# Branch projections of a hybrid encoder layer: another order of weight sums and gate loads, and a sum moved to VectorE

## The reference

```python
y_a = o_a @ w_proj_a[l]      # o_a, o_b: 512 x 1024;  w_proj_a, w_proj_b: 1024 x 2048
y_b = o_b @ w_proj_b[l]
merged = jax.nn.sigmoid(gate_a) * y_a + jax.nn.sigmoid(gate_b) * y_b
x = x + merged @ w_out[l]
```

## Time and profile before

| | us |
|---|---|
| median of 3 runs | 2690.0 |
| the runs | 2689.77 to 2694.65 |
| span of the profiled execution, first to last instruction | 2690.4 |
| TensorE busy in it | 2647.6 (98%) |
| VectorE, ScalarE, GpSimd busy in it | 1820.0, 1374.9, 540.6 |

### The profile page before, as it was taken

How to read it: one execution, slowest core, us unless ns; L and a number is a source line. 1 busy time by engine, 2 the same in 40 slices (tenths; PEclk the granted TensorE clock), 3 DMA queues, 4 the chain that set the end, 5 groups by cost and what they waited for, 6 DMA issues and landing times.

```text
span 2690.4 us, 33239 instructions
## 1 busy us (share of the span) xinstructions
PE 2647.6 (98%) x12726; PEld 2195.0 (82%) x12726; DVE 1820.0 (68%) x2116; ACT 1374.9 (51%) x1692; POOL 540.6 (20%) x390
## 2 busy tenths in 40 slices
PE   8999999999999989999999999999999999999998
PEld 7888888888888778778887888888888888888887
DVE  5865555777666768788458555666655568778787
ACT  6544444645546654545455444444444445544446
POOL 7121112000023222211241122111112212121311
PEclk9999999999999999999999999999999999999999
DMA  8887887532232299875358888787787888798975
GB/s 275 213 196 198 193 184 176 149 89 80 82 92 73 83 256 242 212 200 137 98 157 219 175 170 173 173 198 170 170 179 167 177 213 194 196 208 237 187 213 133
DMA packets 323681, 466.79 MB, mean 174 GB/s; under 512 B 30840, under 2 KB 139728, under 8 KB 320976
## 3 DMA queue, kind: packets, MB, share of 16 engines
q0 software_dynamic: 88672, 170.94, 36.9%
q1 hardware_dynamic: 231936, 288.33, 33.7%
q10 hardware_dynamic: 2928, 5.56, 0.6%
HBM read 430.43 MB, written 34.34 MB: 173 GB/s over the span
## 4 chain that ended last, share of the span: by engine, by line
PE 69%; DVE 4%; DMA 4%; issue 4%; ACT 1%; POOL 1%; DVEq 0%; ACTq 0%; POOLq 0%
PE psum L1186 12%; PE psum L1188 12%; PE psum L1187 12%; PE psum L1607 9%; PE psum L1608 9%; PE psum L1609 9%; DMA f_raw<-in_w_down 1%; PE psum L1369 1%; PE psum L1860 1%; PE psum L1567 1%; PE psum L1568 1%; PE psum L1569 1%; DMA m_tot<-in_w_proj_a 1%; DVE f_lo L3331 1%; DMA out_last<-in_w_out 0%
## 5 line engine op out<-in xcount | busy, mean ns | idle before, releaser
L3552 DVE TENSOR_TENSOR f_lo<-f_raw,f_hi 128x1024 fp32r<-128x1024 f32 x458 | 558.9, 1223 | 398.6 <-ACT f_hi L2572 397.5
L2572 ACT ACTIVATE f_hi<-f_raw 128x1024 fp32r<-128x1024 f32 x460 | 486.6, 1060 | 620.8 <-PE psum L1609 309.8
L1140 POOL DMA_DIRECT2D f_raw<-in_w_up x132 | 158.9, 1204 | 662.3 <-DVE f_lo L3552 619.7
L2893 DVE TENSOR_TENSOR fr_lo<-fr_raw,fr_hi 128x1024 fp32r<-128x1024 f32 x140 | 171.2, 1224 | 158.1 <-ACT fr_hi L2024 157.9
L2024 ACT ACTIVATE fr_hi<-fr_raw 128x1024 fp32r<-128x1024 f32 x140 | 148.4, 1061 | 197.9 <-PE psum L1321 99.7
L1059 POOL TENSOR_TENSOR w_lo<-w_raw,w_hi 128x1024 fp32r<-128x1024 f32 x55 | 136.8, 2502 | 534.6 <-ACT w_hi L1950 526.3
L1186 PE MATMUL psum<-op_hi,w_lo 128*128 128x512 f32 x576 | 233.5, 405 | 0.0
L1188 PE MATMUL psum<-op_hi,w_hi 128*128 128x512 f32 x576 | 224.9, 391 | 0.0
L1187 PE MATMUL psum<-op_lo,w_hi 128*128 128x512 f32 x576 | 224.7, 390 | 0.0
L1159 POOL DMA_DIRECT2D f_raw<-in_w_down x70 | 86.1, 1452 | 285.3 <-DVE f_lo L3552 276.5
L1607 PE MATMUL psum<-f_hi,pa_lo 128*128 128x512 f32 x352 | 137.2, 390 | 0.5 <-DVE f_lo L3552 0.5
(11 more groups left out here) (522 smaller groups left out, 6674.5 us busy)
## 6 DMA issues: line engine op xcount, KB each, us to landing
f_raw<-in_w_up POOLq DMA_DIRECT2D x132, 512.0 KB, 6.6
f_raw<-in_w_gate SPq DMA_DIRECT2D x88, 512.0 KB, 3.8
f_raw<-in_w_down POOLq DMA_DIRECT2D x70, 512.0 KB, 9.1
f_raw<-in_w_down SPq DMA_DIRECT2D x66, 512.0 KB, 5.8
w_raw<-in_w_in SPq DMA_DIRECT2D x64, 512.0 KB, 3.9
fr_raw<-in_w_in SPq DMA_DIRECT2D x60, 512.0 KB, 4.5
fr_raw<-in_w_in POOLq DMA_DIRECT2D x60, 512.0 KB, 7.5
f_raw<-in_w_up SPq DMA_DIRECT2D x44, 512.0 KB, 4.6
```

Of the source, the lines that this page charges most:

```text
L1140: pool.dma_start(raw_pieces(x, slot), up_block(n, p, c), accum_op=ALU.add).then_inc(raw_added[c], 16)
L2572: act.activation(f_split(i)[0][:, :], split_source(i)[:, :], ACT.Copy).then_inc(f_hi_ready, 1)
L2893: dve.tensor_tensor(fr_lo[front_slot(i)][:, :], front_source(i)[:, :], fr_hi[front_slot(i)][:, :].bitcast(F32), ALU.subtract).then_inc(f_l ...
L3552: dve.tensor_tensor(lo[:, :], split_source(i)[:, :], hi[:, :].bitcast(F32), ALU.subtract).then_inc(f_lo_ready, 1)
```

## The change

- GpSimd issues the additions for the third product of block 0, then block 0's fifth-product sum, before the addition for the second product of block 1. It did the last of these first.
- The additions for the seventh products (four blocks, two halves each) are no longer issued by GpSimd. VectorE adds `m_b21` to `m_tot` in place (`last_sums`), for block 0 in steps 10 and 11, for the others in the steps of their sixth product. ScalarE's split of the seventh product waits for that.
- SyncE's four gate loads of block 0 are taken apart: two wait until VectorE has written `m_lo` of the second product's two halves, and two stand behind the load of `m_b22`.
- SyncE's next load of `m_b21` waits for VectorE's sum, since that still reads the tile.
- The counter `f_t_added` has eight more counts, and later users add `MIXED_SUMS`.

```diff
--- before.py
+++ after.py
@@ -111,7 +111,8 @@
 OUT_AT = {step: k for k, step in enumerate(OUT)}
 NO = len(OUT)
 OUT_BLOCKS, OUT_OPERANDS, OUT_SUMS = 28, 14, 8
-F0, TOTALS = FRONT + MIXED, 4 * NF + OUT_SUMS
+MIXED_SUMS = 2 * NG
+F0, TOTALS = FRONT + MIXED, 4 * NF + MIXED_SUMS + OUT_SUMS
 
 
 def out_built_at(operand):
@@ -620,7 +621,7 @@
             n, p, c = mixed_step(i)
             return {3: m_b22, 4: m_low, 5: m_b21}.get(p, m_tot[n % 2])[c]
 
-        TOTAL_ADDS = [(0, 1), (1, 1), (0, 2), (0, 6), (1, 2), (1, 6), (2, 1), (2, 2), (2, 6), (3, 1), (3, 2), (3, 6)]
+        TOTAL_ADDS = [(0, 1), (0, 2), (1, 1), (1, 2), (2, 1), (2, 2), (3, 1), (3, 2)]
 
         def total_added(n, p):
             return 16 * (TOTAL_ADDS.index((n, p)) + 1)
@@ -868,11 +869,17 @@
                 mixed_load(0, "21", c)
             for name in ("11", "12", "21", "22"):
                 sp.wait_ge(S(STORES[name]), front_stored(NF - 1))
-            for name in gate_order(0):
+            def first_gate(name):
                 sp.dma_start(mixed_rows(0, name), gate_block(0, name)).then_inc(S("gate_b_in0"), 16)
+
+            for x in range(2):
+                sp.wait_ge(f_lo_ready, mixed_at(0, 1) + x + 1)
+                first_gate(gate_order(0)[x])
             sp.wait_ge(S("sw_o_done"), HEADS)
             for c in range(2):
                 mixed_load(0, "22", c)
+            for x in range(2, 4):
+                first_gate(gate_order(0)[x])
 
             def gate_b_load(x):
                 n, name = divmod(x, 4)
@@ -888,7 +895,9 @@
                     mixed_load(n, name, c)
 
             for n in range(1, NG):
-                mixed_reload(n, "21", n - 1, 5)
+                for c in range(2):
+                    sp.wait_ge(f_t_added, 4 * NF + 2 * (n - 1) + c + 1)
+                    mixed_load(n, "21", c)
                 mixed_reload(n, "22", n - 1, 3)
                 if n == 1:
                     for name in gate_order(1):
@@ -926,7 +935,7 @@
                     if following < 2:
                         for j in range(4):
                             if freed == 5:
-                                sp.wait_ge(f_t_added, 4 * NF + 4 * q + j + 1)
+                                sp.wait_ge(f_t_added, 4 * NF + MIXED_SUMS + 4 * q + j + 1)
                             else:
                                 sp.wait_ge(f_lo_ready, F0 + OUT_AT[q, freed, j // 2, j % 2] + 1)
                             out_load(following, p, j // 2, j % 2)
@@ -1088,7 +1097,7 @@
                 for c in range(2):
                     chain = S(f"m_added{c}")
                     earlier = total_added(n, p) - 16
-                    used, name = {1: (0, "12"), 2: (1, "22"), 6: (2, "21")}[p]
+                    used, name = {1: (0, "12"), 2: (1, "22")}[p]
                     pool.wait_ge(f_lo_ready, mixed_at(n, used) + c + 1)
                     if earlier:
                         pool.wait_ge(chain, earlier)
@@ -1103,8 +1112,8 @@
 
             for n, p in TOTAL_ADDS:
                 add_total(n, p)
-                if (n, p) == (1, 1) or n and p == 2:
-                    add_low(n if p == 2 else 0)
+                if p == 2:
+                    add_low(n)
 
             def add_out_block(q, p, e, c):
 
@@ -2284,6 +2293,8 @@
                     act.wait_ge(S("m_b21_in"), 32 * (n + 1))
                 elif p == 4:
                     act.wait_ge(S("m_low_added"), 32 * (n + 1))
+                elif p == 6:
+                    act.wait_ge(f_t_added, 4 * NF + 2 * n + c + 1)
                 else:
                     act.wait_ge(S(f"m_added{c}"), total_added(n, p))
                 act.activation(m_hi[slot][:, :], mixed_source(i)[:, :], ACT.Copy).then_inc(f_hi_ready, 1)
@@ -2390,7 +2401,7 @@
                 else:
                     act.wait_ge(f_chunk_done, F0 + k - RING + 1)
                 if p == 6:
-                    act.wait_ge(f_t_added, 4 * NF + 4 * q + j + 1)
+                    act.wait_ge(f_t_added, 4 * NF + MIXED_SUMS + 4 * q + j + 1)
                 elif p in ADDS:
                     act.wait_ge(raw_added[j], 16 * (3 * (q + NF) + ADDS.index(p) + 1))
                 elif p == 0:
@@ -3190,6 +3201,15 @@
                 dve.wait_ge(f_hi_ready, FRONT + i + 1)
                 dve.tensor_tensor(m_lo[slot][:, :], mixed_source(i)[:, :], m_hi[slot][:, :].bitcast(F32), ALU.subtract).then_inc(f_lo_ready, 1)
 
+            def last_sums(i):
+
+                for n in range(NG):
+                    for c in range(2):
+                        if i == (10 if n == 0 else 2 * MIXED_ORDER.index((n, 5))) + c:
+                            o = m_tot[n % 2][c][:, :]
+                            dve.wait_ge(S("m_b21_in"), 32 * (n + 1))
+                            dve.tensor_tensor(o, o, m_b21[c][:, :], ALU.add).then_inc(f_t_added, 1)
+
             def mixed_difference(side, p):
 
                 r11, r12, r21, r22 = ((AR11, AR12, AR21, AR22), (BR11, BR12, BR21, BR22))[side]
@@ -3321,6 +3341,7 @@
                 mixed_low(i)
                 if i in (7, 8):
                     mixed_sum_low(0, i - 4)
+                last_sums(i)
                 mixed_outputs(i)
                 second_operands(i)
```

## The result

| | median us | runs | lowest to highest |
|---|---|---|---|
| kernel before | 2690.6 | 20 | 2685.9 to 2696.1 |
| changed kernel | 2693.5 | 20 | 2692.2 to 2696.8 |

The ratio is 1.0013, with a 95% interval from 1.0007 to 1.0019: slower by 1.9 to 5.1 us. (Ratios here are taken over all runs, each kernel beside the kernel before as it ran with it; they need not be the quotients of the medians.) The forecast was 2688.7 us, 1.3 us faster, with a range to 2693. So the sign was wrong and the time lies 0.5 us beyond the range, though it is within the 0.2% that the prediction called the same. The profiled execution of the changed kernel has a span of 2691.4 us and a time of 2693.2: 1.8 us lie around the span. With the same 1.8 us the first profile of the kernel before, span 2690.4, belongs to an execution of 2692.2 us, not to one of 2690.0.

A forecast was written before the change was run, and what follows sets the result against it. The prediction took TensorE, working in 98% of the span, as the bound, with only its stalls to win back. Winning 10.1 us and giving back 5.9 and 2.9 left 1.3 us won: 2688.7 us, range 2681 to 2693.

The forecast's parts named there:

- old stall: TensorE's 7.2 us wait before step 8 for `m_lo`, plus 2.9 us of half clock: 10.1 us to win.
- new stall: TensorE's wait before step 11, behind VectorE's gate multiplication in step 10: 5.9 us, plus 2.9 us of half clock.
- gates late: Block 0's late gate loads delay step 11 through VectorE's gate multiplication in step 10: 8.8 us given back.
- The third product's sums sooner: Block 0's sums are issued 4.4 and 8.0 us sooner, so the stall before step 8 goes: 10.1 us won.
- TensorE reaches step 11 at 975.1: Without the stall before step 8, TensorE runs three steps of 2.72 us from 966.9 and needs step 11's `m_lo` at 975.1.
- Gate loads later: Block 0's last gate load lands at 978.5, delaying VectorE in step 10 and TensorE before step 11: 8.8 us given back.
- The sums on VectorE: 0: Eight added VectorE instructions of 1.22 us each are covered by its idle time and cost nothing.
- Later loads of `m_b21`: 0, at most 1.5 us: SyncE's wait for VectorE's sums delays loads behind it, in blocks 2 and 3 by 1 to 1.5 us; taken as 0.
- rival (c): Gates land after 979.7, so the stall before step 11 exceeds the one before step 8; up to 2692.0 us; chance 0.20.
- Rival (b): Gates land at 975 to 976.5: a stall of 2.5 to 4 us without half clock, 2682.4 to 2683.9 us; chance 0.17.

The follow-up runs named there:

- e3: Changed kernel with VectorE's product with the first gate of block 0 taken in step 13 instead of step 10, every transfer as changed: 2687.8 us, ratio 0.9989.
- e5: Changed kernel with the edits of e1 and e3 together: 2689.0 us, ratio 0.9992 to the kernel before.
- e7: e6 with GpSimd issuing block 1's second-product sums only after the low parts of block 0's third product: 2682.5 us, ratio 0.9969 to the kernel before.
- e1: Changed kernel with all four gate loads of block 0 early again, as in the kernel before: 2688.2 us, ratio 0.9993.
- e4: Changed kernel with the seventh products' sums back on GpSimd and the reload of their operand waiting as before: 2694.7 us, ratio 1.0014 to the kernel before.
- e2: Kernel before with only the move of block 0's gate loads to later: 2689.1 us, ratio 0.9997.
- e6: e5 with block 1's four gate loads moved behind the first operands of block 2 on SyncE's queue: 2686.1 us, ratio 0.9978 to the kernel before.

## Why the prediction was wrong

The step that failed is the size of the old stall, 10.1 us in the sum and 7.5 measured; smaller errors in the same direction come from the new stall and from small waits later in the stage that the sum had at nothing.

| term of the sum | forecast | measured: mean of the changed kernel less mean of before |
|---|---|---|
| old stall and its clock (steps 7 and 8) | -10.1 | -7.5 |
| gates late (steps 9 to 11) | +8.8 | +9.6 |
| steps 12 to 22 | 0 | +0.8 |
| later loads of `m_b21` (step 49) | 0 | +0.3 |
| steps 3 and 4 | 0 | -0.5 |
| sum | -1.3 | +2.6 |

**The third product's sums sooner.** The mechanism was right: step 8 began at 966.91, where 966.9 was forecast, without a wait. The size failed: the term of -10.1 us measured -7.5, and this is the largest error of the sum, 2.6 us. The 10.1 us were read from one execution, and its stall was the longest of four, which range from 4.8 to 9.9 us. The times shown beforehand, 2689.8 to 2694.7, already spread by 5 us, as much as half the stall. That the base was taken from the median while the stall was taken from one profile belongs to the same error: that execution, at 2692.2 us by its span, stood 1.6 us above the median of 20 runs (though a long stall does not by itself make a long time, as the second profile shows).

**TensorE reaches step 11 at 975.1.** This step failed too: the wait for `m_b22` before step 10 put it 1.3 us later (973.65 against 966.9 + 2 x 2.72 = 972.3). It cost nothing here, because the gate was later still; once the gate's wait was cured, in e3 and e5, it was what remained, and e7 shows its cause. The stall before step 11 measured 5.88 us, where 5.9 was forecast, by luck: TensorE came 1.3 us later than forecast, and the gates landed 1.5 us later.

**Gate loads later.** Right in kind and place, and in that the clock fell to 0.50 again (from 983 to 987 us): VectorE's product in step 10 ended its wait with the transfer into `rows_m`, step 11's `m_lo` stood behind it, and e1 and e3 each take the loss away. The landing was 980.0 instead of 978.5, at the slow bound of 980.1 taken from the old gate loads, where the slowest took 19.7 us and now 19.8. The shares of the queues were nearly right: the two loads of `m_b22` and the two late gates landed at 967.0, 971.1, 975.1 and 980.0, 4.0 to 4.9 us apart, where the prediction's working has 966.5 and then 4.0 us each. (Its 1.5 us ahead of the first and 2.3 behind the last are together 3.8 us, more than the whole 3.7 us load that they were taken from.) The clock cost 2.5, 2.0 and 2.3 us instead of 2.9. Together 9.6 instead of 8.8, of which 1.2 is the wait before step 10. The Trainium skill, page "DMA: Bandwidth & Descriptors", section "Anatomy of one DMA — SWDGE (gpsimd) path", gives 2.0 us and the bytes at 436 KB per us for a transfer on GpSimd's path; taken for SyncE's loads, as in the prediction, it has the four land at an estimated 965.5. The trace does not agree for loads beside adding transfers, 19.8 us for the last.

**The sums on VectorE: 0.** Right as far as it can be measured: e4, without them, has the same ratio, 1.0014 against 1.0013.

**Later loads of `m_b21`: 0, at most 1.5 us.** Left open. Step 49 lost 1.6, 1.0 and 1.4 us in the changed kernel, but 0.6, 2.6, 0 and 0.9 in the kernel before, and 1.6 in e2, where the loads of `m_b21` stand as before. No part of it can be put down to the change.

**What was not in the sum.** Steps 12 to 22 lose 0.6 to 1.0 us in the changed kernel and nothing in the kernel before. The largest part of this stands before step 19, where TensorE waits for `m_lo` of block 1's third product (0.46 us in the second profile); the same wait is longer in e3 and e5, and e6 shows that block 1's gate loads beside the sums caused it there. That they cause it in the changed kernel too is not shown.

**The rivals.** What happened is nearest to rival (c): a landing behind 979.7, slower than before. But the landing alone doesn't make the loss: with 980.0 for 978.5 and all else as forecast, the prediction's sum comes to 980.0 + 2.5 - 975.1 + 2.9 - 10.1 = 0.2 us slower; the size of the old stall makes most of the rest. (Rival (c)'s own 2.0 us add up to 1.8.) Its chance of 0.20 was too low, since the point from which it decides lay 1.2 us from an estimate whose bounds lay 8 us apart, and a smaller old stall would have moved that point to an earlier landing. The range ended at 2693, but the end of (c) that it was said to leave out began at 0.2%, 2695.4 us: 2693.5 lies in between, in a stretch that was given no chance of its own. Rival (b), a short stall without the half clock, would not have come out as priced: e2's wait of 3.49 us cost 1.6 us of clock behind it, that of 2.93 us in the second profile of the kernel before 1.7.

## What to carry over

A stall that ends with a transfer can have a size that varies from one execution to the next: the old one cost 4.8 to 9.9 us in four profiles, though the new one, which ends with a transfer too, cost 8.4 to 8.6 in three. Before a stall is entered in a sum as what can be won, profile the same kernel a few times, and take stall and base from the same executions. When a load is moved later, look for the first instruction that waits for it and for what stands behind that one on its engine: moving that instruction won about as much here as moving the load back. Look also at the count that it waits for: here two waits, for the gates and for `m_b22`, were for more blocks than the instruction reads. And where the DMA engines are full, holding back a transfer that nobody needs yet brings the needed one in sooner: two such moves, block 1's gates and block 1's sums, took the ratio to the kernel before from 0.9992 to 0.9969.

## What the runs showed of the hardware

The same idle time did not always cost the same clock. In the second profile of the kernel before, TensorE waited 1.81 us before step 4, and the granted clock fell to 0.88 in the stretch that holds the wait and 0.84 in the next; the step took 5.62 us. In the third the wait was 1.82 us, the clock stayed at 1.00, and the step took 4.04. The stretches from 952 to 964 us of the second, then of the third profile (columns as above):

```profile
952.00:958.00 6.00, 4.19 (x20) 3.33 (x19) 3.68 (x4) 2.60 (x3) 3.69 (x3) 0.88 1.11 250
958.00:964.00 6.00, 6.00 (x50) 4.62 (x50) 0.00 (x0) 2.56 (x4) 2.41 (x2) 0.84 1.09 189
```

```profile
952.00:958.00 6.00, 4.18 (x23) 3.35 (x22) 4.11 (x5) 2.90 (x4) 3.69 (x3) 1.00 1.10 251
958.00:964.00 6.00, 6.00 (x55) 4.79 (x54) 0.27 (x1) 3.40 (x4) 2.41 (x2) 1.00 1.11 199
```

Plain loads on SyncE's queue and adding transfers on GpSimd's slowed each other down: an adding transfer landed 4.0 us sooner when four plain loads were moved away from beside it (e6), and a plain load took 9.9 instead of 12.2 us when two adding transfers were (e7).
